# Two latent norms folded into the work behind them, and layer norm sums taken earlier, in a two-block transformer kernel on one core

## The chip, the cores and the metric

The kernel runs on one core of one Trainium2 chip. The metric is the device time of one execution in microseconds; less is better. Engines are named as in the profile: PE multiplies matrices (PEld loads its weights beside it), DVE and ACT work on vectors, POOL is the general engine, SP issues the DMAs. An operand is "f32" or "fp32r", the form in which a float32 value is split in a high part and a low part, so that one product is made of three matrix instructions.

## The reference, cut to what matters

Two blocks of two layers each are computed for 512 tokens of width 1024. The change touches the second block. Its layers are a state-space mixer with a gated feed-forward part, and a latent attention with a gated feed-forward part. Each of these four parts ends in a layer norm. In the latent attention both norms are root-mean-square norms:

```python
ckv_kr = h @ kv_down_proj                                  # 256 latent columns and 64 for the rotated key
c_kv   = rms_norm(ckv_kr[..., :256], kv_norm_g)
k_rope = apply_rope(ckv_kr[..., 256:], cos, sin)
k_nope, v = c_kv @ kv_up_k, c_kv @ kv_up_v                  # 8 heads of 128
c_q    = rms_norm(h @ q_down, q_norm_g)                     # 384 latent columns
q      = c_q @ q_up                                         # 8 heads of 128 + 64 rotated
scores = (q_nope @ k_nope.T + q_rope @ k_rope.T) * 192 ** -0.5
p      = softmax(where(key <= query, scores, -inf))
o      = (p @ v) @ out_proj
h      = layer_norm(alpha * h + o, g, b)                    # also behind the other three parts
```

A factor that belongs to one query (the reciprocal root of its mean square) multiplies all of that query's scores, so it may be applied to the scores as well as to the latents.

## The kernel before, in words

**Layout.** Activations lie transposed: 128 partitions hold 128 features, the 512 tokens are the columns, and 8 tiles make the width of 1024. A sum over features is therefore a product with a column of ones (`ones`), which gives one value per token, with tokens on the partitions; to spread a value per token over the partitions again, PE transposes it.

**Weights.** They stream through a ring of six slots. SP loads a slab, ACT copies it to the high part (`wh`, L486), POOL subtracts to get the low part (`wl`, L494), and PE multiplies three times (L520 to L522, the helper `product`). `split.hi(n)` and `split.lo(n)` do this for all slabs before number n, on ACT and POOL, at the place in the program where they stand. A slot is loaded again when the product that read it is done. Every engine works through its own list in program order and waits on semaphores; there is no other order.

**Latents.** Class `Latents` makes six tiles from the last layer norm's output: key-value latents 0 and 1, the rotary key (tile 2, its 64 rows twice), and query latents 0 to 2. Tiles 0 to 3 are the "head" of the crossing before, tiles 4 and 5 follow. DVE first computes the angles of sine and cosine, 16 small steps in all, then copies all six tiles out of PSUM. PE turns the rotary key (`rot2`, L1987), then comes the key-value norm and then the query norm, each as: square on ACT, sum by PE (L937), mean on DVE, power on POOL (L978), a diagonal matrix on DVE (L971), spread by PE (L962), multiply on DVE (L2059). After both, ACT makes the high parts and DVE the low parts of the five latent tiles and the rotary key, ACT writes zeros into the unused halves of the rotary key's tiles (L2015, L2016), and only behind all this does ACT convert the first slabs of the next stage (L486, four of them) and POOL make their low parts.

**LatentAttention.** Before its loop over eight heads PE projects, for the first head or pair, the rotary queries, the plain queries, turns the rotary part (L2162), then the keys and the values. A head is: scores (L520 and following), maximum on DVE (L2273), exponential on ACT (L2198, its scale a constant, its bias a value per partition), division by the sum on DVE (L2281), transposes of the probabilities on PE (L1507), and the products of the head before with the values. The projections of the next head stand between scores and transposes.

**Layer norm.** The `Dense` product before each layer norm is made of eight output tiles; the last one or two, the tail, are done in two halves of the tokens by a `Crossing`, so that the next stage can begin on the first half. To keep the squares small, tiles 0 and 1 give an estimate of the mean (`shift_sum`, L670, and `shift_spread`, L677), which is subtracted from all tiles. Then POOL adds the tiles up (L784, L775) in `gather`, ACT squares each (L711) into `tmp`, and DVE adds the squares up (L717) in `gather2`. `LayerCrossing.stat` (L1428) sums both over the features with PE; it waits for the tail's last square, which DVE adds at L1268, and for the last addition into `gather` (POOL's L775, DVE's L1418). `spread` (L1439) sends the result back, and DVE, ACT and POOL make the next stage's input from it (L1480, L1486, L1451, L1452, L1307). `STAT, SPREAD` say after which of the second half's weight rows in the tail these two stand. There are four such norms: behind the state-space mixer (three of its tiles are begun early, `early`, and its tail has two tiles), behind the first feed-forward part (tail of one tile), behind the latent attention (tail of two), and behind the last feed-forward part (tail of one).

## Time and profile before

| | |
|---|---|
| median of 3 runs | 2695.4 us (2692.55 to 2701.34) |
| the profiled execution's own time | 2694.61 us |
| its span in the profile | 2692.8 us |
| instructions | 32522 |
| PE busy | 2593.2 us, 96% of the span |
| POOL, DVE and ACT busy | 1175.0, 1376.2 and 1092.2 us |
| latents to first scores | 2096.3 to 2142.3 us of the span |
| layer norm behind the state-space mixer, tail to next stage | 1670.4 to 1699.4 us |
| layer norm behind the latent attention, tail to next stage | 2285.1 to 2306.4 us |

A row of a timeline gives the start in the span, the duration, the engine and line, the operation and its operands, a count where like instructions are merged, and in brackets how long the engine had been idle before and what ended that. A row of windows gives a stretch, then each engine's busy time in it, the granted PE clock as a share of 2.4 GHz (0.50 is the lower of its two levels, 1.2 GHz), the DMA engines' share and GB/s.

### The profile page before, as it was taken

How to read it: one execution, taken by the hardware profiler on the slowest of the kernel's cores; microseconds unless marked ns; L12 is line 12 of the kernel's file. 1: busy time of each engine (PE TensorE's matmuls, PEld its weight loads, DVE VectorE, ACT ScalarE, POOL GpSimd, SP SyncE). 2: the span in 40 equal slices, each digit the busy share in tenths (PEclk: the TensorE clock that was granted, in tenths of full speed). 3: DMA queues.
4: the chain of work that ended last, by engine and by line, in shares of the span. 5: the costliest groups of instructions: out<-in, count | busy, mean ns of one | idle time of the engine just before them, and what ended most of it. 6: DMA issues, size and time to landing. Idle time of an engine off the chain costs nothing.

```text
span 2692.8 us, 32522 instructions
## 1 busy us (share of the span) xinstructions
PE 2593.2 (96%) x13188; PEld 2187.5 (81%) x13188; DVE 1376.2 (51%) x2096; ACT 1092.2 (41%) x1885; POOL 1175.0 (44%) x634
## 2 busy tenths in 40 slices
PE   7999999999999999998999999899999899999997
PEld 5887988888889888896888887788888688888886
DVE  6775540523435505237574665661644574661654
ACT  5554531324225313324463554532434453542432
POOL 3333663444455644443334333544446214544443
PEclk9999999999999999998999999899999899999998
DMA  5222333332333333322223222223323112223332
GB/s 150 62 68 57 91 98 94 98 98 68 105 94 94 94 95 101 94 80 56 63 71 86 66 68 63 72 83 112 98 86 83 34 53 76 71 84 112 94 90 67
DMA packets 436005, 224.26 MB, mean 83 GB/s; under 512 B 14864, under 2 KB 433936, under 8 KB 435856
## 3 DMA queue, kind: packets, MB, share of 16 engines
q1 hardware_dynamic: 435856, 222.18, 29.0%
q8 instruction: 104, 1.70, 0.3%
q14 instruction: 45, 0.37, 0.0%
HBM read 219.01 MB, written 2.10 MB: 82 GB/s over the span
## 4 chain that ended last, share of the span: by engine, by line
PE 91%; DVE 5%; ACT 2%; POOL 1%; issue 1%; DMA 0%; SPq 0%; POOLq 0%; DVEq 0%; ACTq 0%
PE ps L520 28%; PE ps L522 28%; PE ps L521 28%; PE ps L2523 1%; PE ps L2509 1%; PE ps L1507 1%; PE ps L1428 1%; PE ps L2530 0%; PE ps L2511 0%; DMA xT<-in_xT 0%; ACT tmp L1664 0%; POOL sm L1821 0%; DVE acc L1486 0%; PE ps L2548 0%; DVE tmp L2766 0%
## 5 line engine op out<-in xcount | busy, mean ns | idle before, releaser
L494 POOL TENSOR_TENSOR wl<-stg,wh 128x1024 fp32r<-128x1024 f32 (+4 forms) x447 | 1003.7, 2252 | 1256.5 <-ACT wh L486 1249.8
L520 PE MATMUL ps<-hh,wh 128*128 128x512 f32 (+1 forms) x2308 | 868.7, 376 | 31.5 <-POOL wl L494 10.2
L522 PE MATMUL ps<-hh,wl 128*128 128x512 f32 (+1 forms) x2308 | 856.9, 371 | 0.0
L521 PE MATMUL ps<-hl,wh 128*128 128x512 f32 (+1 forms) x2308 | 856.3, 371 | 0.0
L486 ACT ACTIVATE wh<-stg 128x1024 fp32r<-128x1024 f32 (+4 forms) x447 | 435.6, 984 | 307.2 <-DMA stg<-in_mlp_w_down 109.2
L520 PEld LDWEIGHTS ps<-hh,wh 128*128 128x128 f32 x2308 | 436.8, 189 | 111.5 <-issue 17.2
L522 PEld LDWEIGHTS ps<-hh,wl 128*128 128x128 f32 x2308 | 436.4, 189 | 75.7
L521 PEld LDWEIGHTS ps<-hl,wh 128*128 128x128 f32 x2308 | 437.2, 189 | 72.3 <-issue 1.2
L520 PE MATMUL ps<-bh,wh 128*128 128x512 f32 (+1 forms) x1304 | 488.0, 374 | 2.4 <-DVE bl L1783 1.6
L522 PE MATMUL ps<-bh,wl 128*128 128x512 f32 (+1 forms) x1304 | 484.4, 371 | 0.0
L521 PE MATMUL ps<-bl,wh 128*128 128x512 f32 (+1 forms) x1304 | 484.3, 371 | 0.0
L520 PEld LDWEIGHTS ps<-bh,wh 128*128 128x128 f32 x1304 | 248.2, 190 | 45.0 <-DVE bl L1783 2.0
L522 PEld LDWEIGHTS ps<-bh,wl 128*128 128x128 f32 x1304 | 247.8, 190 | 42.3
L521 PEld LDWEIGHTS ps<-bl,wh 128*128 128x128 f32 x1304 | 248.0, 190 | 41.1
L884 DVE TENSOR_TENSOR bl<-tmp,bh 128x512 fp32r<-128x512 f32 x64 | 140.4, 2193 | 51.5 <-ACT bh L874 51.5
L1952 DVE SCALAR_TENSOR_TENSOR tmp<-ps,vec,tmp 128x511 f32<-128x511 f32 x88 | 66.0, 750 | 156.2 <-ACT tmp L1937 155.9
L1937 ACT ACTIVATE tmp<-ps,vec 128x512 f32<-128x512 f32 x88 | 67.7, 771 | 145.4 <-PE ps L522 145.2
L796 DVE COPY acc<-ps 128x512 f32<-128x512 f32 (+1 forms) x36 | 22.7, 632 | 182.2 <-PE ps L522 182.2
L869 ACT ACTIVATE tmp<-ps 128x512 f32<-128x512 f32 x64 | 38.1, 595 | 182.1 <-PE ps L522 182.1
L2766 DVE SCALAR_TENSOR_TENSOR tmp<-ps,vec,tmp 128x511 f32<-128x511 f32 (+2 forms) x96 | 71.9, 748 | 73.2 <-ACT tmp L2622 71.0
L881 DVE TENSOR_TENSOR tmp<-tmp 128x512 f32<-128x512 f32 x64 | 56.7, 886 | 94.0 <-ACT tmp L869 94.0
L1960 DVE SCALAR_TENSOR_TENSOR tmp<-tmp 128x512 f32<-128x512 f32 x44 | 91.2, 2073 | 0.0
(305 smaller groups left out, 2734.3 us busy)
## 6 DMA issues: line engine op xcount, KB each, us to landing
stg<-in_ffn_up SPq DMA_DIRECT2D x88, 512.0 KB, 3.8
stg<-in_mlp_w_up SPq DMA_DIRECT2D x64, 512.0 KB, 4.0
stg<-in_mlp_w_down SPq DMA_DIRECT2D x64, 512.0 KB, 4.0
stg<-in_ssd_in_proj SPq DMA_DIRECT2D x48, 512.0 KB, 3.9
stg<-in_attn_w_qkv SPq DMA_DIRECT2D x24, 512.0 KB, 4.1
stg<-in_conv_w_in SPq DMA_DIRECT2D x24, 512.0 KB, 3.7
stg<-in_ffn_down SPq DMA_DIRECT2D x32, 384.0 KB, 3.3
stg<-in_ffn_down SPq DMA_DIRECT2D x32, 320.0 KB, 3.1
```

Of the source, the lines that this page charges most:

```text
L486: act.activation(wh[:, slab.slot, w], stg[:, slab.slot, w], ACT.Copy).then_inc(s.hi_done, 1)
L494: pool.tensor_tensor(wl[:, slab.slot, w], stg[:, slab.slot, w], wh[:, slab.slot, w].bitcast(F32), ALU.subtract).then_inc(s.lo_done, 1)
L520: pe.matmul(po, lh, rh, start=start, stop=False)
L521: pe.matmul(po, lh, rl, start=False, stop=False)
L522: return pe.matmul(po, ll, rh, start=False, stop=stop)
L869: act.activation(tmp[:, t % 2, :], ps[:, t, :], ACT.Relu).then_inc(s.bank_free, 1)
L881: dve.tensor_tensor(tmp[:, 2 + t % 2, :], tmp[:, t % 2, :], tmp[:, t % 2, :], ALU.mult).then_inc(s.squared, 1)
L884: dve.tensor_tensor(tile(bl, 4 * i + t), tmp[:, 2 + t % 2, :], tile(bh, 4 * i + t).bitcast(F32), ALU.subtract).then_inc(s.hid_lo, 1)
L1937: act.activation(tmp[:, 3 * u + n, :], ps[:, 2 * u + n, :], ACT.Identity, bias=v("ffn_b", 2 * i + (self.b0 + n * FFN_T + u)), scale=self.t ...
L1952: dve.scalar_tensor_tensor(y[:, 1:T], x[:, 0:T - 1], self.taps(n, 1, i, u), y[:, 1:T], ALU.mult, ALU.add).then_inc(s.ffn_tap, 1)
L1960: dve.scalar_tensor_tensor(gate, th, 1.0, gate, ALU.add, ALU.mult).then_inc(s.ffn_silu, 1)
L2766: op = dve.scalar_tensor_tensor(y[:, d:T], x[:, 0:T - d], self.conv_col(i, n, 3 - d), y[:, d:T], ALU.mult, ALU.add)
```

## The change

- **Order and place of the latents.** Query tiles stay in PSUM banks 3, 1 and 2 (`Q_BANK`); only three tiles are copied. Tile 4 goes to bank 1 and so waits for two of the copies. The key-value sums stand inside tile 4's product, the key-value spread inside tile 5's; the spread is four transposes and no longer a diagonal matrix. The second half of the angle steps moves behind the copies.
- **Query norm.** The query latents are multiplied by the gain only. Their sums (`query_sums`) stand among the first projections. The factor of each query times 192 ** -0.5 becomes `q_scale`, a value per partition, which scales the exponential (and the maximum, by one `scalar_tensor_tensor` where a `tensor_scalar` stood).
- **Key-value norm.** The two normed tiles go to `bh`, `bl` tiles 6 and 7, so that they need not wait for the last product that reads `hh`.
- **Keys first.** The stage's slabs come as key, rotary, plain, value; PE's order is the same. ACT and POOL convert these four slabs (`split.hi`, `split.lo` up to `st.end + LEAD`) ahead of the query squares and behind the key-value power. The zeros of the rotary key's tiles come last on ACT.
- **Layer norm sums.** Squares go to two PSUM banks that are free instead of `tmp`. Without `early`, the estimate's sum stands inside tile 2's product and its spread at the head of tile 3's, and the order of shifts and squares becomes 2, 0, 1, 3. With `early`, POOL adds up four tiles only, and `stat` sums the other four with PE directly; `STAT, SPREAD` become 11 and 15. With two tail tiles, DVE's addition at L1418 falls away, and PE sums that tile too. So `stat` has six parts behind the state-space mixer and four behind the latent attention, where it had three; behind the feed-forward parts it keeps three.

```diff
+            st_mla = (stage("latent attention begin", 1, [(2, P, lambda i: key(0, 0)), (3, P, rope),
+                                                          (3, P, lambda i: nope(0, 0)), (2, 2 * P, value)]),
...
+            if self.shift and not self.early and n == 2 and x0 == 0:
+                return lambda j: self.shift_sum(pe) if j == 5 else None
+            if self.shift and not self.early and n == 3 and x0 == 0:
+                return lambda j: self.shift_spread(pe) if j == 0 else None
...
-            dve.tensor_tensor(gather2, gather2, tmp[:, 4 + k % 2, :], ALU.add).then_inc(s.sq_sum, 1)
+            dve.tensor_tensor(gather2, gather2, self.square_place(k), ALU.add).then_inc(s.sq_sum, 1)
...
+            self.f1 = dense.f0 + dense.summed()
+            if dense.early:
+                self.STAT, self.SPREAD = 11, 15
...
-        def tail_sum(self, dve, half, n):
-            super().tail_sum(dve, half, n)
-            if n < DT_ - 1:
-                k, cols = self.number(half, n), half_columns(half)
-                dve.wait_ge(s.gathered, self.f1 + half)
-                dve.tensor_tensor(gather[:, cols], gather[:, cols], acc[:, n, cols], ALU.add).then_inc(s.gathered, 1)
...
+            parts = [(gather, 0)] + [(acc[:, n, :], 0) for n in range(self.dense.summed(), DT_)] + [(gather2, 2)]
...
         def tensor(self, pe):
-            for pos in (4, 5):
-                multiply(pe, self.st, pos, 0, ps[:, pos, :], hh, hl, 0)
-            pe.wait_ge(s.kvq_copied, 4)
-            pe.matmul(ps[:, 3, :], rot2, acc[:, 2, :], start=True, stop=True).then_inc(s.kr_rot, 1)
-            self.kv.tensor(pe)
-            self.q.tensor(pe)
+            def rows(j):
+                if j == 5:
+                    for n in range(2):
+                        self.kv.stat(pe, n)
+            pe.wait_ge(s.kvq_copied, 2)
+            multiply(pe, self.st, 4, 0, ps[:, 1, :], hh, hl, 0, ready=rows)
+            pe.wait_ge(s.kvq_copied, 3)
+            pe.matmul(ps[:, 0, :], rot2, acc[:, 2, :], start=True, stop=True).then_inc(s.kr_rot, 1)
...
+                if j == 1:
+                    end.then_inc(s.lat_rows, 1)
+                if j == 2:
+                    self.spread(pe)
...
+            act.wait_ge(s.ang_done, 16)
+            act.activation(self.cos, tmp[:, 3, :], ACT.Sin).then_inc(s.tab_done, 1)
+            split.hi(act, self.st.end + LEAD)
+            wait_product(act, self.st, 4, 0)
...
+            for pos in range(3):
                 wait_product(dve, self.st, pos, 0)
                 dve.tensor_copy(acc[:, pos, :], ps[:, pos, :]).then_inc(s.kvq_copied, 1)
+            angle(1)
...
         def tensor(self, pe):
+            pe.wait_ge(s.kvq_lo, 4)
+            self.project_key(pe, 0)
+            pe.wait_ge(s.kvq_lo, 5)
+            pe.wait_ge(s.kr_done, 1)
+            self.project_rope(pe, 0)
+            self.lat.query_sums(pe)
+            self.project_nope(pe, 0)
+            self.turn(pe, 0)
+            pe.wait_ge(s.cross_var, self.lat.v0["cross_var"] + 2)
+            self.project_value(pe, 0)
             pe.wait_ge(s.kvq_lo, 7)
             pe.wait_ge(s.kr_zero, 4)
-            self.project_rope(pe, 0)
-            self.project_nope(pe, 0)
-            self.turn(pe, 0)
-            self.project_key(pe, 0)
-            self.project_value(pe, 0)
...
-                               bias=nm[:, n:n + 1], scale=self.scale,
+                               bias=nm[:, n:n + 1], scale=Latents.q_scale[:, b:b + 1],
```

## Rows read from the trace of the kernel before

**Rows 1.** The page's part 1: busy time, share, instructions.
```profile
PE 2593.2 (96%) x13188; PEld 2187.5 (81%) x13188; DVE 1376.2 (51%) x2096; ACT 1092.2 (41%) x1885; POOL 1175.0 (44%) x634
```
**Rows 2.** Waits of PE in the span: total us, times, longest.
```profile
PE ps L1428 <- DVE cb L1268: 18.5, 3, 11.8
...
PE ps L520 <- POOL wl L494: 10.2, 3, 8.1
```
**Rows 3.** Window from the last latent product to the first of the next stage.
```profile
2107.25:2131.50 24.25, 11.76 (x47) 8.50 (x46) 12.14 (x20) 9.99 (x18) 3.15 (x4) 0.57 0.02 6
```
**Rows 4.** Timeline of PE: tile 4's start, turn, two sums, first scores.
```profile
2096.33 0.40 PE L520 MATMUL ps<-hh,wh 128*128 128x512 f32 x1
...
2107.25 1.02 PE L1987 MATMUL ps<-acc,con 128*128 128x512 f32 x2
2108.11 1.84 PE L937 MATMUL ps<-con,tmp 128*128 128x1 f32 x16
...
2114.20 5.12 PE L937 MATMUL ps<-con,tmp 128*128 128x1 f32 x24
...
2142.34 0.40 PE L520 MATMUL ps<-bh 128*128 128x512 f32 x1
```
**Rows 5.** Timeline of DVE in the latents: end of the first angle, the copies.
```profile
2095.54 0.43 DVE L2042 TENSOR_SCALAR tmp<-tmp 128x512 f32<-128x512 f32 x1
...
2100.02 3.08 DVE L2046 COPY acc<-ps 128x512 f32<-128x512 f32 x5
```
**Rows 6.** Timeline of ACT and POOL: the four slabs of 1536 columns.
```profile
2129.76 1.76 ACT L486 ACTIVATE wh<-stg 128x384 fp32r<-128x384 f32 x4
...
2130.36 3.90 POOL L494 TENSOR_TENSOR wl<-stg,wh 128x384 fp32r<-128x384 f32 x4 [9.76 <-ACT wh L486]
```
**Rows 7.** Windows of the two stalled crossings: wait, then sums to next stage.
```profile
1678.75:1690.39 11.64, 0.00 (x0) 0.03 (x1) 8.05 (x7) 4.29 (x7) 11.64 (x6) 0.58 0.00 0
1690.39:1699.35 8.96, 8.96 (x46) 8.80 (x47) 2.76 (x10) 1.48 (x3) 1.57 (x2) 0.59 0.20 59
...
2293.12:2297.21 4.09, 0.00 (x0) 0.03 (x1) 3.49 (x4) 0.39 (x1) 4.09 (x3) 0.74 0.00 0
2297.21:2306.36 9.15, 9.15 (x47) 9.15 (x47) 2.96 (x11) 1.48 (x3) 1.56 (x2) 0.56 0.20 57
```
**Rows 8.** Timeline of the state-space crossing: first sum, POOL's last addition, DVE behind it.
```profile
1673.28 1.72 DVE L717 TENSOR_TENSOR cb<-cb,tmp 128x512 f32<-128x512 f32 x1
...
1685.21 1.25 POOL L775 TENSOR_TENSOR cb<-cb,acc 128x512 f32<-128x512 f32 x1
...
1686.50 2.55 DVE L1418 TENSOR_TENSOR cb<-cb,acc 128x256 f32<-128x256 f32 x1 [2.25 <-POOL cb L775]
```
**Rows 9.** Groups of DVE by form, 2060 to 2400: busy, mean ns.
```profile
L2286 DVE TENSOR_TENSOR bl<-ps,bh 128x512 fp32r<-128x512 f32 x16 | 11.0, 690 | 10.3 <-ACT bh L2210 8.1 <-ACT bh L2214 2.0
L717 DVE TENSOR_TENSOR cb<-cb,tmp 128x512 f32<-128x512 f32 x7 | 10.3, 1470 | 2.1 <-ACT tmp L711 2.1
```
**Rows 10.** Feed-forward crossing: PE's spread and next stage, then a window.
```profile
2066.79 0.43 PE L1439 MATMUL ps<-con,sm 128*128 128x128 f32 x2
...
2070.09 0.55 PE L520 MATMUL ps<-hh,wh 128*128 128x256 f32 x1 [1.94 <-DVE hl L1307]
...
2073.00:2074.00 1.00, 1.00 (x9) 1.00 (x9) 0.97 (x3) 1.00 (x3) 0.49 (x1) 0.88 0.00 0
```
**Rows 11.** Groups of ACT by form, 2060 to 2400: a pointer operand, none.
```profile
L2198 ACT ACTIVATE acc<-ps,sm 128x512 f32<-128x512 f32 x8 | 5.5, 688 | 17.9 <-DVE sm L2275 17.9
...
L2210 ACT ACTIVATE bh<-ps 128x512 fp32r<-128x512 f32 x8 | 4.8, 604 | 9.9 <-PE ps L522 9.9
```
**Rows 12.** A head in the loop: last division, first transpose.
```profile
2202.36 0.36 DVE L2281 TENSOR_SCALAR acc<-acc,sm 128x256 f32<-128x256 f32 x1
...
2205.10 0.38 PE L1507 MATMUL ps<-con,acc 128*128 128x128 f32 x2
```
**Rows 13.** The page's part 6: DMA issues, KB each, us to landing.
```profile
stg<-in_ffn_up SPq DMA_DIRECT2D x88, 512.0 KB, 3.8
```

More of the change, by code:

```diff
@@ L603, in begin, with summed @@
             self.early, self.banks = count, banks
+        def summed(self):
+            return TB if self.early else self.full
         def bank_of(self, n):
@@ L701, in square_order, with square_place @@
         def square_order(self):
-            return [2, 3, 0, 1] + list(range(4, self.full))
+            return ([2, 3, 0, 1] if self.early else [2, 0, 1, 3]) + list(range(4, self.full))
+        def square_place(self, k):
+            return ps[:, ((0, 1) if self.parts > 1 else (2, 3) if self.early else (5, 6))[k % 2], :]
         def shifted_square(self, act, n):
@@ L729, in shifted_vector, with shifted_vector_early @@
             self.shift_mean(dve)
+            dve.wait_ge(s.gathered, self.f0 + 1)
+            if self.early:
+                return self.shifted_vector_early(dve)
+            self.shift_tile(dve, 2)
+            self.shifted_out(dve, 2)
+            for n in (0, 1, 3):
+                self.shift_tile(dve, n)
+            for n, done in ((4, 2), (5, 0), (6, 1)):
+                self.shift_tile(dve, n)
+                self.shifted_sum(dve, done)
+            self.shift_tile(dve, 7)
+            for n in range(3, self.full):
+                self.shifted_out(dve, n)
+                self.shifted_sum(dve, n)
+        def shifted_vector_early(self, dve):
             for n in (2, 3):
@@ L1182, in bank_free @@
             pe.wait_ge(s.acc_done, SEED + d.before + max(users, default=1))
+            if d.shift and d.parts == 1 and not d.early:
+                for k in range(d.full - 2, d.full):
+                    if self.bank[half, n] == 5 + k % 2:
+                        pe.wait_ge(s.sq_sum, SEED + d.g0 + k + 2)
         def head_products(self, pe, half):
```

217 lines of the change are left out of this document (128 added, 89 removed).

## The prediction

> **What bounds the kernel.** I read the busy times first: PE is busy for 2593.2 of 2692.8 us [rows 1], so some 100 us of it is idle, and only work that PE does, its clock, or those gaps can give anything. The waits of PE come next. The largest is L1428, the layer norm's sums, 18.5 us in three places, of which 11.8 in one (4.1 is in the second [rows 7], so 2.6 in the last); the wait for the first low weights of the latent attention costs 8.1 [rows 2]. These are the places that the change touches. The windows then show what the waits cost beside the idle time: from 2107.25 to 2131.50 PE is busy for 11.76 of 24.25 us at a mean clock of 0.57 [rows 3], and behind both stalled sums it works at 0.59 and 0.56 [rows 7]. Everything else in these stretches has to be followed engine by engine, since each engine works in its own order. For the unit costs: 48 matrix instructions of 512 columns took 2107.25 - 2096.33 = 10.92 us [rows 4], so 0.2275 each, and I take half of this, about 0.12, for 256 columns. Sixteen instructions of one column took 1.84 us [rows 4]; they are two sums over four token blocks, so a tile's sum costs 0.92, and one part of a `stat` (two blocks) 0.46.
>
> **Part A, the latents.** I place each engine's list anew from 2096.33, where tile 4 starts now [rows 4]. DVE has done the first angle at 2095.97 [rows 5]; its copies cost 3.08 / 5 = 0.62 each, so banks 0 and 1 are out at 2097.3. PE waits 1.0 for them: a new stall. Then:
> - tile 4, 24 x 0.2275 = 5.46, the key-value sums inside it 1.84, the turn 0.86 (to the next start [rows 4]): 2105.5. Tile 5 with 0.4 for the transposes: 5.86, to 2111.35.
> - DVE has the second angle (2095.97 to 2100.02 [rows 5], so 4.0) behind the copies, at 2101.9. ACT stands at the cosine until then; behind it wait the four slabs (1.76 [rows 6]), which are high at 2104.4, and the squares of query tiles 0 and 1. POOL's power, an estimate of 1.0 us under the 1.25 of a whole operation [rows 8], and its four low slabs (3.90 [rows 6]) are done at 2107.8, before the keys need them. The 8.1 us wait is gone, since the slabs no longer stand behind the zeros.
> - The spread lands at 2108.0. DVE's chain to the low key-value tiles is two norms, two query lows and two lows, six operations of about 0.69 [rows 9]: 2112.2. PE waits 0.9. Keys 6 x 0.2275: 2113.65.
> - Rotary key cosine and sum, then the low part of query tile 2: DVE at 2114.2; PE waits 0.6. Rotary queries 2.05, query sums 3 x 0.92, plain queries 2.05: 2121.1. The third square can start only after the first sum, and the sum of tile 2 comes right behind it, with nothing lost.
> - ACT still has the third square and four zeros (0.55 each, an estimate from the 0.60 of a whole tile [rows 11]) ahead of the high keys and the raw rotary queries; these end at 2121.4, so the turn waits 0.4. Turn 0.9, values 24 x 0.12 = 2.9: 2125.3. DVE's rotation and the low rotary queries (four operations with two waits on ACT between) end at 2126.1. The scores start at 2126.2.
>
> Against 2142.34 [rows 4] that is 16.1 us less, of which 3.8 is left in five small stalls; without any stall it would be 20, the upper bound. The lower bound is the clock. In the trace a wait of 1.94 us let the clock fall, and it was back only in the window 2073 to 2074 [rows 10], three microseconds later, which costs 1.5. The one-column sums also do nothing to bring it up: at 2114.20 twelve logical sums took 5.12 us, with waits, and the window's mean stayed 0.57 [rows 3, 4]. I charge one such fall, 1.5: **A = -14.6**, between -18 and, with the clock low for most of the dense work, -5. Here a rule of the skill speaks for the better case. The Trainium skill, "TensorE: Matmul & The Clock Gate", What's actually happening, says the slow clock is the default and the engine's recent business releases it; if sums counted as business, A would be -16.1. The rows above do not show the sums releasing it.
>
> **Part B, the exponential's scale.** The exponential gets a second value per partition. Operations of 512 columns out of PSUM take 604 ns without one and 688 with one [rows 11], so 0.08 more for each of 32. The function differs between the two rows, which leaves the price of the second open: nothing at the least, and 0.69 if it doubled the operation. In the loop the last division ends 2.4 us before PE needs it (2202.72 against 2205.10 [rows 12]); four times 0.08 lies in that. Only in the last head, where no projection covers the chain, it shows: +0.3. If the cover were gone in all heads, it would be 2.6; doubled, the operations would take 2.8 a head, 0.4 beyond the cover, and 3 to 5 in all. The maximum's operation stays one instruction of one column. The slabs of the loop keep the order in which PE uses them.
>
> **Part C, the sums behind the state-space mixer.** Now POOL adds tiles 4 and 5 between its weight slabs and ends at 1686.46 [rows 8], DVE adds the tail tile only after that and beside POOL, in 2.55 us [rows 8], and PE starts the sums at 1690.39, 11.6 after it was there [rows 7]. After the change POOL's additions end with tile 3, two additions (1.3 each) and two slabs earlier; a slab of 1024 columns is 2.6 by rows 6 (3.90 for 1536), so before 1679, when PE is not there yet. DVE's sums read PSUM and cost 0.69 where they cost 1.47 [rows 9]. That the two slow each other is what the Trainium skill says too ("GPSIMD Engine Reference", Specifications: the interface is shared when DVE has two SBUF inputs); it changes no term here. What is late next is the tail's last square. DVE's sums begin at 1673.3 as now [rows 8]; the first four alternate with ACT's squares until 1676.0. ACT then copies four slabs (1.05 to 1.2 each, from 1.76 for 1536 columns [rows 6]) and squares tiles 4 and 5 (0.6 each), so it reaches the tail's first square at about 1680.6 to 1681.6. Two squares, two outputs and two sums of a half tile follow, and the last sum is in at about 1682.5. PE comes to `stat`, now after 12 of 16 rows, at 1680.6: a wait of 2. Then six parts instead of three, 2.8 us at full clock. POOL's four low slabs (2.5 each, begun with ACT's first copy at 1676.5) end at about 1686.5, and the power behind them lets the spread go at 1687.3 at the earliest, 1689.8 if the clock has fallen. From spread to the next stage it takes 2070.09 - 2066.79 = 3.3 [rows 10], and no tail rows are left to cover it. The next stage starts at 1692.5 with 1.5 either way, 6.9 before 1699.35 [rows 7]. The second half's `stat` adds 6 x 0.23 = 1.4, and I charge 1.0 for a low clock in the next stage: **C = -4.5**, between -2.5 and -7.4.
>
> **Part D, the sums behind the latent attention.** The estimate moves ahead by most of a tile's product (24 x 0.2275 = 5.5), so shifts, squares and sums keep pace with PE, and DVE's 2.5 us addition of the tail falls away. The last slab that ACT copies needs the slot of tile 5, free at 2285.1, and 3.8 for its DMA [rows 13]; it stands ahead of the tail's square, which so comes at 2290.1. I get the last sum at 2292.3, before PE is there at 2293.1 [rows 7]. So the 4.1 us wait is gone, and with it the low clock behind it. From there: four parts 1.84, four rows 1.45, waiting for the spread 0.35, then 3.3: 2300.0, against 2306.36 [rows 7], -6.4; the second half's additional part costs 0.5. **D = -5.9**, between -4 (the copy late by one DMA) and -6.5.
>
> **Part E, the two feed-forward norms.** The estimate's sum after 15 of a tile's first 18 instructions finds POOL's first addition done: 15 x 0.2275 = 3.4 us after the tile before it, in which DVE needs 0.69 and POOL 1.25, with one slab of 2.0 at most in its way. Nothing waits for the squares there but the tail, whose wait is on its own half. Zero; if POOL were late by a slab, half a microsecond each.
>
> **The sum.** -14.6 + 0.3 - 4.5 - 5.9 = -24.7. The profiled execution took 2694.6 us, 1.8 outside its span, so 2669.9; the median of the runs is 0.8 above it. I say 2670.
>
> **Rivals.**
> - *The clock never falls in the new stretches.* A -16.1, C -7.4, D -5.9, +0.3: -29.1, 2666. For it: none of the new stalls in A is above 1.0, where the fall in the rows came with 1.94 [rows 10]. Against: 4.6 us of one-column sums and several stalls in 30 us. Chance 0.17. The rule of the Trainium skill quoted in part A ("TensorE: Matmul & The Clock Gate", What's actually happening) would lead here.
> - *The clock stays low through the latents and the state-space crossing.* Some 15 us of dense work in A takes nearly twice as long, partly inside the stalls: A -5, C -2.5, D -5.9: -13, 2682. For it: before, the mean was 0.57 for 24 us [rows 3]. Against: PE was then busy half the time, now 0.85 of it. Chance 0.15.
> - *The sums' gain is taken up by POOL.* `power` stands on POOL behind the four low slabs, and if these run until 1690 as now (POOL is busy for all 11.64 [rows 7]), the spread waits where `stat` waited. C is then 0 to +1.4, D -2: with A and B at -14.3 that is some -15.5, 2679. Against: POOL loses two additions and starts earlier. Chance 0.08.
> - *Slower.* The exponential with a pointer scale costs much more than the rows of the other functions tell, and the softmax chain, which has 2.4 us of cover per head, comes to set the loop. To lose 8 us in all it must eat 24.7 + 8 over eight heads, 4.1 each behind the cover of 2.4: 1.6 us more per exponential, where the pointer rows say 0.08. It gives 2703 at that point. Chance 0.02.
> - *The latents' gain is real but small for another reason*, such as ACT's cosine wait holding slabs and squares longer than I placed them; around 2678. Chance 0.05, and 0.53 for the forecast.
>
> **Range.** A measurement of this kernel tells 0.3%, 8 us, from no change. The forecast's own range is 2666 to 2676. The first rival lies at its lower edge and the next ones reach 2682; from 2661 to 2683 no more than 0.1 is left out on either side. Faster by over 0.3% 0.95, within it 0.03, slower 0.02.
>
> **What would show it.** The scores of the first head start near 2126 to 2128, with no PE wait on L494 above 1 us before them and small waits ahead of tile 4, keys, rotary queries and turn. The two L971 and L962 groups are gone there. The first `stat` of the state-space crossing waits about 2 us, that of the latent attention not at all; the last one, 2.6 us, stays. L717 takes 0.7 us. The exponentials take 0.08 more, and the distance from head to head stays. The prediction is wrong if the granted clock is 0.5 in the dense work of A, if ACT is what `stat` waits for by 5 us, or if a head becomes longer.

## The result, and the profile of the changed kernel

The changed kernel takes 2670.95 us (median of five, four of them from 2670.64 to 2673.07) against 2695.4 us. The fifth was in a slow state, 3250.5 us at a mean granted clock of 0.75; without it the median is 2670.9, and nothing below is taken from it. The ratio is 0.9906 with a 95% interval of 0.9892 to 0.9921: 0.9% faster. 2670 was forecast. Measured a second time beside the kernel before, the ratio was the same (below).

The page of the profiled execution, head and busy times (before: [rows 1]):

```profile
span 2671.2 us, 32576 instructions
PE 2595.1 (97%) x13220; PEld 2189.2 (82%) x13220; DVE 1348.6 (50%) x2085; ACT 1094.3 (41%) x1885; POOL 1168.2 (44%) x632
```

PE is busy for 1.9 us more than before; its idle time fell from 99.6 to 76.1 us, and the span is 21.6 us shorter. The changed kernel's waits of PE, some of the rows (before: [rows 2]):

```profile
PE ps L523 <- DVE hl L1334: 6.2, 6, 2.6
...
PE ps L1452 <- DVE cb L1295: 4.2, 2, 2.6
...
PE ps L523 <- DVE bl L2406: 3.5, 3, 1.8
```

The layer norm's sums, 18.5 us of waiting before, cost 4.2, and the 8.1 us for the first low weights of the latent attention are gone. In the latents, the timeline of PE has these waits (before, one of 8.1 us and a clock of 0.57 beside it: [rows 2 to 4]):

```profile
2111.06 0.50 PE L523 MATMUL ps<-bh,wh 128*128 128x512 f32 x1 [0.59 <-DVE bl L2133]
...
2113.05 0.50 PE L523 MATMUL ps<-hh,wh 128*128 128x512 f32 x1 [0.32 <-DVE hl L2090]
...
2120.17 0.70 PE L2253 MATMUL ps<-tmp,con 128*128 128x512 f32 x1
...
2124.97 0.47 PE L523 MATMUL ps<-bh 128*128 128x512 f32 x1 [0.80 <-DVE bl L2399]
```

The turn (2120.17) waits for nothing; the keys, the rotary queries and the scores wait 0.59, 0.32 and 0.80 us. Tile 4, ahead of these rows, waits 0.86. The windows of the same kernel over the latents, and over the crossing behind the latent attention:

```profile
2095.25:2110.30 15.05, 14.19 (x70) 11.49 (x70) 9.18 (x17) 9.05 (x15) 4.91 (x5) 1.00 0.25 66
2110.30:2124.97 14.67, 12.94 (x75) 10.37 (x75) 8.20 (x15) 7.90 (x15) 1.39 (x2) 1.00 0.17 45
2271.00:2296.00 25.00, 23.84 (x199) 23.27 (x198) 13.26 (x38) 13.19 (x24) 13.77 (x13) 1.00 0.22 63
```

PE is busy for 14.19 of 15.05 us and 12.94 of 14.67, at full clock throughout. Behind the latent attention the clock holds too. It does not hold behind the state-space mixer. First PE's timeline there:

```profile
1684.36 0.58 PE L1452 MATMUL ps<-con,cb 128*128 128x1 f32 x4 [1.62 <-DVE cb L1295]
1684.80 2.42 PE L1452 MATMUL ps<-con,acc 128*128 128x1 f32 x16
1687.08 0.99 PE L1452 MATMUL ps<-con,cb 128*128 128x1 f32 x4
1687.93 0.56 PE L523 MATMUL ps<-bh,wh 128*128 128x256 f32 x1
...
1690.63 0.63 PE L1463 MATMUL ps<-con,sm 128*128 128x128 f32 x2
...
1694.33 0.55 PE L523 MATMUL ps<-hh,wh 128*128 128x256 f32 x1 [2.64 <-DVE hl L1334]
```

Then the windows of the same stretch (before: [rows 7]):

```profile
1678.49:1682.70 4.21, 4.21 (x36) 4.04 (x34) 1.82 (x4) 4.06 (x6) 4.21 (x2) 1.00 0.03 8
...
1684.36:1687.95 3.59, 3.59 (x25) 3.59 (x25) 0.00 (x0) 0.00 (x0) 3.50 (x2) 0.74 0.03 9
1687.95:1694.33 6.38, 3.74 (x17) 3.37 (x18) 2.71 (x10) 1.48 (x3) 0.71 (x1) 0.50 0.29 82
1694.33:1702.24 7.91, 7.91 (x48) 7.91 (x49) 4.26 (x12) 5.52 (x11) 2.20 (x3) 0.66 0.00 0
1702.24:1708.12 5.88, 5.88 (x39) 5.88 (x39) 2.59 (x8) 3.02 (x5) 4.75 (x6) 0.71 0.00 0
```

PE waits 1.62 us for the last sum; then 24 one-column instructions take 3.7 us. In the middle of them, at 1686.0, the clock falls to 0.50 for 13.65 us, and at 1703.1 for 3.41 us more.

**How runs are compared below.** The total moves by several microseconds from one execution to the next, and most of that lies early. The profiles show it: VectorE's MEMSET that opens the layer norm behind the state-space mixer starts anywhere between 1654.20 and 1665.34 us in thirteen profiles, although almost no kernel changes anything ahead of it (the two that do are named; the changed kernel and the one before run the same instructions up to there). From there on, two executions of the changed kernel agree within 0.2 us in every stretch. So I read each profile from that MEMSET (M) on, in stretches between instructions that all kernels have: to the first variance of the first feed-forward crossing (F1), its second (F2), the first row maximum of the latent attention (X), the second variance behind it (V), the end. All numbers are differences of start times in us, the last is taken to the end of the span. There is one profile of each kernel and two of the changed one, so a difference that comes from one row alone can be one of execution.

| kernel | M to F1 | F1 to F2 | F2 to X | X to V | V to end | M to end |
|---|---|---|---|---|---|---|
| before | 408.68 | 10.65 | 68.19 | 167.33 | 381.43 | 1036.28 |
| changed | 406.08 | 10.06 | 52.21 | 162.96 | 381.42 | 1012.73 |
| changed, again | 406.07 | 10.07 | 52.23 | 162.95 | 381.40 | 1012.72 |
| lat_only | 408.67 | 10.76 | 52.21 | 168.71 | 380.88 | 1021.23 |
| sums_only | 406.09 | 10.06 | 68.17 | 161.27 | 380.86 | 1026.45 |
| nm_pointer | 405.95 | 10.08 | 53.34 | 161.90 | 381.49 | 1012.76 |
| const_scale | 406.06 | 10.08 | 52.19 | 159.71 | 381.46 | 1009.50 |
| tail_order | 403.86 | 11.15 | 54.97 | 164.08 | 381.23 | 1015.29 |
| fill_idle | 402.66 | 10.08 | 52.20 | 162.90 | 381.48 | 1009.32 |
| zeros_first | 406.06 | 10.07 | 51.86 | 163.22 | 381.39 | 1012.60 |
| pool_late | 405.93 | 10.07 | 53.33 | 158.22 | 381.42 | 1008.97 |
| split_sums | 405.44 | 10.08 | 52.20 | 163.11 | 381.43 | 1012.26 |
| combined | 402.37 | 10.07 | 51.83 | 161.04 | 380.80 | 1006.11 |

Between the first two rows lie 23.55 us: 2.60 behind the state-space mixer, 0.59 in the feed-forward crossing, 15.98 in the latents, and 4.37 in the heads and the crossing behind them. The 2 us by which the two spans differ less (21.6) were lost ahead of M.

### The profile page after: what moved, and what is told of

It is laid out like the page before. It is cut to its first block, busy times and chain, and to the rows that moved or that the text cites. A ratio compares the mean times of both kernels' runs of the same rounds, so it can differ in the third digit from the quotient of the medians.

```text
span 2671.2 us, 32576 instructions
## 1 busy us (share of the span) xinstructions
PE 2595.1 (97%) x13220; PEld 2189.2 (82%) x13220; DVE 1348.6 (50%) x2085; ACT 1094.3 (41%) x1885; POOL 1168.2 (44%) x632
## 4 chain that ended last, share of the span: by engine, by line
PE 92%; DVE 5%; ACT 1%; POOL 1%; issue 1%; DMA 0%; SPq 0%; DVEq 0%; POOLq 0%; ACTq 0%
PE ps L523 29%; PE ps L525 28%; PE ps L524 28%; PE ps L2622 1%; PE ps L2608 1%; PE ps L1452 1%; PE ps L1531 1%; PE ps L2629 0%; DVE acc L1510 0%; PE ps L1554 0%; DMA xT<-in_xT 0%; PE ps L2610 0%; DVE acc L1504 0%; ACT tmp L1688 0%; POOL sm L1845 0%
## 5 line engine op out<-in xcount | busy, mean ns | idle before, releaser
L523 PE MATMUL ps<-hh,wh 128*128 128x512 f32 (+2 forms) x2292 | 864.2, 377 | 29.3 <-DVE hl L1102 11.2
L525 PE MATMUL ps<-hh,wl 128*128 128x512 f32 (+2 forms) x2292 | 851.8, 372 | 0.0
L524 PE MATMUL ps<-hl,wh 128*128 128x512 f32 (+2 forms) x2292 | 851.4, 371 | 0.0
L523 PEld LDWEIGHTS ps<-hh,wh 128*128 128x128 f32 (+1 forms) x2292 | 435.0, 190 | 107.8 <-issue 21.3
L523 PE MATMUL ps<-bh,wh 128*128 128x512 f32 (+1 forms) x1320 | 493.8, 374 | 2.9 <-DVE bl L1807 1.6
L525 PEld LDWEIGHTS ps<-hh,wl 128*128 128x128 f32 (+1 forms) x2292 | 434.8, 190 | 74.8
L524 PEld LDWEIGHTS ps<-hl,wh 128*128 128x128 f32 (+1 forms) x2292 | 435.5, 190 | 71.6 <-issue 1.2
L525 PE MATMUL ps<-bh,wl 128*128 128x512 f32 (+1 forms) x1320 | 489.8, 371 | 0.0
```

Source lines behind the costliest of these rows:

```text
L523: pe.matmul(po, lh, rh, start=start, stop=False)
L524: pe.matmul(po, lh, rl, start=False, stop=False)
L525: return pe.matmul(po, ll, rh, start=False, stop=stop)
```

## The experiments

### One part of the change alone

Two kernels, each the kernel before with one part of the diff. `lat_only` has the stage order, `Latents` and `LatentAttention`; `sums_only` has `Dense`, `LayerCrossing` and their places for squares. The core of each:

```diff
 # lat_only
-                               bias=nm[:, n:n + 1], scale=self.scale,
+                               bias=nm[:, n:n + 1], scale=Latents.q_scale[:, b:b + 1],
...
 # sums_only
+            if dense.early:
+                self.STAT, self.SPREAD = 11, 15
```

> The kernel before with only the latent and attention edits (keys first, query norm in the exponential's scale); the layer norms' sums as before. Theory A (the ledger of the two profiles holds part by part, and the parts add): 16.1 us less to the first scores, 1.5 to 1.8 us given back in the heads, so 14.3 to 14.6 us under the kernel before, near 2681. Rival (part of what the ledger puts down to the latents was granted clock that happened to be better in that one execution, or the gains overlap with those of the sums): at most 12 us, 2683 or more. In the trace: second stall of the latents gone, first scores 16 us earlier, the crossing behind the state-space mixer as before.

> The kernel before with only the edits of the layer norms' sums; latents and attention as before. Theory A (ledger): 2.6 us behind the state-space mixer and 6.0 behind the latent attention, 8.6 in all, near 2686.8. Rival 1 (the prediction's own terms, 4.5 and 5.9): 10.4, near 2685.0. Rival 2 (feed-forward crossings lose or gain too because squares now go through PSUM banks): another 0.5 us either way beyond 8.6, seen in those crossings' windows.

Measured: `lat_only` 2687.26 us, ratio to the kernel before 0.9952 (0.9937 to 0.9967), which is 12.9 us; `sums_only` 2690.78 us, ratio 0.9970 (0.9959 to 0.9980), 8.1 us. The intervals, 9 to 17 and 5 to 11 us, hold both the theory and the rival of each, so the totals decide nothing. From M to the end they are 15.05 and 9.83 us shorter than the kernel before, 24.9 together, where the whole change has 23.55. The latents' stretch is 15.98 shorter in `lat_only`, as in the whole change, and the stretch behind the state-space mixer 2.59 shorter in `sums_only`. So the parts add within 1.4 us, and most of that lies in the last stretch, V to end, where both took 0.55 less and the changed kernel, which has both edits, did not; up to V they add to 23.8 against 23.5. `lat_only` changes nothing in that stretch. In `sums_only` 2.59 and 6.06 us are the 8.6 of theory A, and the 0.59 in the first feed-forward crossing is what its second rival allowed for. Two further readings follow. The heads with the crossing behind them take 1.38 us more in `lat_only` than before and 1.69 more in the changed kernel than in `sums_only`: that is what part B cost in these executions, the clock included. And the same stretch puts part D at 6.06 in `sums_only`, and at 5.75 between `lat_only` and the changed kernel.

### The maximum's operation in the last head

Part B was forecast at 0.3 us. VectorE's timeline of the changed kernel in the last head shows two operations of one column that take over 1 us; the group of all 32 has a mean of 222 ns. Below them GpSimd's slab operations at that time:

```profile
2221.83 1.07 DVE L2371 SCALAR_TENSOR_TENSOR sm<-sm 128x1 f32<-128x1 f32 x1
...
2224.05 1.20 DVE L2371 SCALAR_TENSOR_TENSOR sm<-sm 128x1 f32<-128x1 f32 x1
...
2225.49 0.16 DVE L2371 SCALAR_TENSOR_TENSOR sm<-sm 128x1 f32<-128x1 f32 x1
...
2220.50 2.39 POOL L497 TENSOR_TENSOR wl<-stg,wh 128x1024 fp32r<-128x1024 f32 x1
2222.84 2.40 POOL L497 TENSOR_TENSOR wl<-stg,wh 128x1024 fp32r<-128x1024 f32 x1
```

Both long operations end with a slab: 2221.83 + 1.07 = 2222.90 and 2220.50 + 2.39 = 2222.89; 2224.05 + 1.20 = 2225.25 and 2222.84 + 2.40 = 2225.24. Without a slab beside it the same operation takes 0.16. PE, which needs what follows from it for the transposes, waits 2.05 us:

```profile
2228.21 1.90 PE L1531 MATMUL ps<-con,acc 128*128 128x128 f32 x10 [2.05 <-DVE acc L2378]
```

Three kernels ask whose fault that is.

```diff
 # nm_pointer: one tensor operand, the query scale as a scalar operand
-                dve.scalar_tensor_tensor(nm[:, n:n + 1], mx[:, n:n + 1], -1.0, Latents.q_scale[:, b:b + 1], ALU.mult,
-                                         ALU.mult).then_inc(s.m_negmax, 1)
+                dve.tensor_scalar(nm[:, n:n + 1], mx[:, n:n + 1], Latents.q_scale[:, b:b + 1], -1.0, ALU.mult,
+                                  ALU.mult).then_inc(s.m_negmax, 1)
 # const_scale: the maximum times -self.scale, and in the exponential
-                               bias=nm[:, n:n + 1], scale=Latents.q_scale[:, b:b + 1],
+                               bias=nm[:, n:n + 1], scale=self.scale,
 # pool_late: GpSimd in the attention stage
+            split.lo(pool, self.st[2].end + lead(self.st[2]) - 2)
+            pool.wait_ge(s.m_combined, 4 * HEADS)
             lo_stage(pool, self.st[2])
```

> The changed kernel, with the row maximum's operation written as one tensor-scalar operation: the maximum times the query scale as the scalar operand, times minus one; one tensor operand in SBUF instead of two, same result. Theory A (an operation with two SBUF tensor operands waits for GpSimd's slab operations, which run beside it in the last head): the 1.07 and 1.20 us operations fall to 0.15 to 0.2, the last head gets shorter by about 1 us on VectorE, and the time falls by 0.5 to 1.5 us against the changed kernel, to 2669.5 to 2670.5. Rival (the long records are a coincidence of that execution, or hidden behind the exponentials): same time as the changed kernel, 2671, within 0.3 us.

> The changed kernel with the constant scale in the exponentials and in the maximum's operation, so the query norm's factor is left out of the softmax. Theory A (the pointer scale costs 0.09 us in each exponential, of which only the end of a head and of the loop sees any, and the maximum's operation costs 1 us in the last head): 1.3 to 1.8 us under the changed kernel, near 2669.3. Rival 1 (the prediction's term, 0.3 us): 2670.7. Rival 2 (the 1.8 us that the heads took more are clock or upstream delay, not the operations): exponentials at 0.69 us again, the heads' stretch no shorter.

> The changed kernel; GpSimd waits with the last two of the three slabs that it splits beside the last head until that head's normalising is through. Theory A (a VectorE operation from SBUF to SBUF that starts beside a GpSimd slab operation is held until that one ends, as 2221.83 + 1.07 and 2224.05 + 1.20 in the changed kernel fall on the ends of slab operations): the maximum's operations take 0.16 us in the last head, the wait ahead of its transposes is 1.0 instead of 2.05 us, and with the better clock 1.0 to 1.6 us less; nothing waits for the two slabs. Rival (the operation is slow for another reason, as its pointer operand): still over 1 us, nothing gained; or the output projection waits for the late slabs and gives it back.

Measured: `nm_pointer` 2675.04 us, ratio to the kernel before 0.9911 (0.9891 to 0.9932); `const_scale` 2673.26 us, ratio 0.9912 (0.9892 to 0.9931); `pool_late` one run, 2675.61 us, with M at 1664.83, late by itself. Against the changed kernel at 0.9906 none of these totals tells anything, and none of the gains that were expected of them shows in them; the stretches tell more. The last head of `nm_pointer`, VectorE and then GpSimd:

```profile
2228.78 0.21 DVE L2371 TENSOR_SCALAR sm<-sm 128x1 f32<-128x1 f32 x1
...
2231.88 1.70 DVE L2378 TENSOR_SCALAR acc<-acc,sm 128x512 f32<-128x512 f32 x1
...
2230.91 2.38 POOL L497 TENSOR_TENSOR wl<-stg,wh 128x1024 fp32r<-128x1024 f32 x1
```

The maximum's operation no longer waits for a slab, as theory A has it: 0.21 us beside GpSimd. But 3 us later the first normalising of the probabilities, 0.49 us in the changed kernel, is caught instead and takes 1.70, until 0.29 after the slab's end at 2233.29. PE's wait ahead of the transposes is 2.38 us instead of 2.05, so the operations' gain didn't reach PE. The stretch X to V is 1.06 shorter all the same; PE's first scores of that head ran at full clock here and not in the changed kernel, so no part of it is put down to the edit. The same rows of `pool_late`:

```profile
2228.06 0.16 DVE L2371 SCALAR_TENSOR_TENSOR sm<-sm 128x1 f32<-128x1 f32 x1
2229.22 0.56 DVE L2369 TENSOR_REDUCE sm<-ps 128x1 f32<-128x384 f32 x1 [1.00 <-PE ps L525]
2229.82 0.16 DVE L2371 SCALAR_TENSOR_TENSOR sm<-sm 128x1 f32<-128x1 f32 x1
...
2231.01 0.49 DVE L2378 TENSOR_SCALAR acc<-acc,sm 128x512 f32<-128x512 f32 x1
...
2232.96 2.36 POOL L497 TENSOR_TENSOR wl<-stg,wh 128x1024 fp32r<-128x1024 f32 x1 [5.06 <-DVE acc L2378]
...
2232.93 1.31 PE L1531 MATMUL ps<-con,acc 128*128 128x128 f32 x10 [1.02 <-DVE acc L2378]
```

With the slabs held back, the unchanged operation with its two SBUF inputs takes 0.16 us throughout that head, the normalising 0.49, and PE waits 1.02 us instead of 2.05, as expected. X to V is 4.74 us shorter than in the changed kernel, more than the 1.0 to 1.6 expected. Not all of that is the edit's: already ahead of it, from 2218.20 to 2222.53, the changed kernel's clock was 0.61, and `pool_late`'s stayed at 1.00. In `combined`, where the clock fell there again, the same edit is left with 1.9 us, so its worth lies between 1.9 and 4.7. That stretch of `combined` is also no longer than that of `sums_only` (161.04 against 161.27), with two falls of 3.41 us of the clock in both: with the slabs out of the way the new scale costs nothing there. And in all eight profiles in which PE waits 2.0 us or more ahead of those transposes, the clock is then low for 6.8 us or longer, in the other five for 3.4 or not at all; so I read part B's price as the longer wait and the low clock that comes with it. The wait varies from one execution to the next: in `tail_order`, which changes nothing there, the two operations took 2.19 and 1.84 us and PE waited 3.64.

In `const_scale`, which leaves the query norm's factor out of the softmax and so computes something else, the exponentials take 0.69 us again where the changed kernel has 0.78 (512 columns), and the wait ahead of the transposes is 0.98. X to V is 3.25 us shorter than in the changed kernel and 1.56 shorter than in `sums_only`, in which the same operations stand: there the clock fell a second time. So the two prices of B can't be had from this kernel to better than one fall of the clock.

The Trainium skill, "SBUF — State Buffer", Who interferes with whom, states the rule that I should have weighed: a DVE operation with both inputs in SBUF contends with GpSimd's reads, a copy or `tensor_scalar` can too in a two-port mode, and whoever comes second is blocked until the first has finished. The rows agree, to 0.01 us in the first two cases; for the normalising, with one tensor input, they agree with its second half.

### The clock behind the state-space mixer

```diff
 # tail_order, ScalarE and VectorE
-            split.hi(act, self.split_at + self.ahead())
+            early = self.dense.early
+            split.hi(act, self.split_at + self.ahead() - (1 if early else 0))
             for n in self.tail:
                 self.tail_square(act, 0, n)
+            split.hi(act, self.split_at + self.ahead())
...
+            if self.dense.early:
+                for n in self.tail:
+                    self.tail_out(dve, 0, n)
+                for n in self.tail:
+                    self.tail_sum(dve, 0, n)
 # fill_idle, 12 ahead of the first stat and 18 ahead of the next stage
+            for _ in range(count):
+                pe.matmul(po, wh[:, slot, 0:po.shape[0]], self.dense.xh[:, 0, 0:256], start=True, stop=True)
 # split_sums
-                        self.stat(pe, 1)
+                        self.stat(pe, 1, (0, 1, 2))
+                    if half == 0 and j == 2 and self.dense.shift and self.dense.early:
+                        self.stat(pe, 1, (3, 4, 5))
```

> The changed kernel; in the crossing behind the state-space mixer VectorE first evicts both tail tiles' first halves and then adds their squares, and ScalarE squares them ahead of its last slab copy. Theory A (the wait of 1.62 us ahead of the first sums is this chain alone, and with it goes the half clock in which the 24 one-column products and 12 rows ran): wait under 0.5 us, sums in 2.4 to 2.8 us instead of 3.71, clock 1.00 up to the spread, next stage's first product 3 to 4.5 us earlier after the crossing's start, and about 3 us less in all. Rival (the half clock comes from the sums themselves, one-column products, not from the wait): the wait goes, the sums still take 3.7 us, next stage 1.2 to 1.6 us earlier.

> The changed kernel; in the crossing behind the state-space mixer TensorE runs 12 products of 256 columns into a free bank ahead of the first sums, and 18 ahead of the next stage's first product; their results are overwritten or never read. No other engine is changed. Theory A (the clock fell because TensorE stood idle there, and the fall is what made this term smaller than predicted): clock 1.00 through the crossing, sums 2.4 to 2.8 us instead of 3.71, next stage's products and the second sums at full clock, 2 to 4 us less up to the second half's variance and the stage behind it. Rival (one-column products lower the clock whatever stands before them, or the chain over VectorE and GpSimd sets the times): clock falls all the same or the times stand still, at most 0.5 us less.

> The changed kernel; the second sums behind the state-space mixer are issued as 12 one-column products behind the next stage's second tile and 12 behind its third instead of 24 in a row, and the 24 of the query's squares in the latents as 8 ahead of each of the three column blocks of the first content query. Seen so far: right behind the 24 in a row of the second sums the clock fell in every run with the new sums (the stretch from the second variance to the next crossing takes 362.1 us, 360.65 before), and behind the 24 of the query in three runs of eight (1.1 to 2.8 us). Theory A (a long unbroken row of one-column products counts for the clock as little work): with the rows broken up the clock stays at 1.00 behind both, the stretch from the second variance falls from 362.1 to 360.7 to 361.2 us, the latents' stretch is 52.2. Rival (the stretch is longer because the second variance now comes earlier against the same products, or the clock fell from the idle time ahead): 362 us again, or what is saved behind the sums is lost because the variance comes 0.7 us later.

One run each: 2671.25, 2670.10 and 2671.28 us. The first two edits also reached the one crossing of this kind in the first block, ahead of M; there the filling cost 2.7 us. Their windows from the last tail products on, first `tail_order`:

```profile
1678.70:1681.51 2.81, 2.81 (x25) 2.81 (x26) 0.00 (x0) 0.19 (x1) 2.81 (x3) 1.00 0.53 156
1681.51:1688.65 7.14, 3.45 (x17) 2.78 (x17) 4.47 (x10) 1.48 (x3) 2.84 (x2) 0.53 0.26 73
```

The wait is 0.21 us instead of 1.62, and the sums take 2.81 instead of 3.7. Yet right behind them the clock is down (0.53), without any idle time ahead of them but that 0.21. M to F1 is 2.2 us shorter, not 3, and the next stage starts 1.4 us earlier, not 3 to 4.5; theory A was right on the wait and on the sums and wrong on the clock and on the start, which came as the rival has it. `fill_idle`:

```profile
1683.23:1684.86 1.63, 1.44 (x14) 1.26 (x12) 1.03 (x3) 0.39 (x1) 1.63 (x2) 1.00 0.99 292
1684.86:1687.66 2.80, 2.80 (x25) 2.80 (x26) 0.00 (x0) 0.00 (x0) 2.80 (x2) 1.00 0.01 3
1687.66:1692.99 5.33, 4.35 (x35) 3.97 (x35) 3.11 (x10) 1.48 (x3) 1.49 (x2) 1.00 0.34 98
1692.99:1699.48 6.49, 5.93 (x49) 5.73 (x50) 4.27 (x12) 5.52 (x11) 2.20 (x3) 1.00 0.01 3
1699.48:1705.22 5.74, 5.74 (x37) 5.74 (x37) 2.60 (x8) 3.03 (x5) 4.75 (x6) 0.70 0.00 0
```

Thirty instructions whose results nobody reads, and the clock stays at 1.00 for 16 us; M to F1 is 3.42 us shorter than in the changed kernel. The edit touches no other engine, so I read this as what the 13.65 us of low clock cost in this stretch. The last row shows that the fall behind the second sums is still there, and ahead of it PE had not been idle for more than 0.56 us at a time. `split_sums` breaks up those sums:

```profile
1693.05:1698.51 5.46, 5.46 (x27) 5.46 (x27) 4.26 (x12) 5.06 (x11) 2.21 (x3) 0.51 0.00 0
1698.31:1702.51 4.20, 4.20 (x38) 4.20 (x38) 0.00 (x0) 0.65 (x2) 0.00 (x0) 0.99 0.00 0
1702.51:1706.15 3.64, 3.06 (x25) 2.86 (x25) 2.59 (x8) 2.23 (x5) 2.86 (x5) 1.00 0.00 0
```

Behind the two groups of 12 the clock is 1.00, where it was 0.71 behind the 24 in a row. All nine profiles with the 24 second sums in a row have that fall, and neither of the two with groups (`split_sums`, `combined`). The stretch from the second variance to F1 falls from 362.13 to 360.03, as theory A has it; but the second variance comes 1.4 us later against the first, and M to F1 is only 0.64 shorter: the rival's second half is true as well. The fall at the first sums, which this edit leaves in a row, is still there. The query sums were broken up too, but their stretch of 52.20 us is what most profiles have without that, so it shows nothing.

### The last stall of the latents, and the clock there

```diff
-            self.q.square(act, 2, ps[:, self.Q_BANK[2], :])
             for e in range(2):
                 other = slice(64 - 64 * e, 128 - 64 * e)
...
+            self.q.square(act, 2, ps[:, self.Q_BANK[2], :])
...
+            self.rope(dve, 0)
             self.low(dve, 0, 1, self.QN, ps[:, 5, :])
-            self.rope(dve, 0)
             self.rope_low(dve, 0)
```

> The changed kernel; in the latents ScalarE writes the four zero halves of the rotary keys ahead of the third query square, and VectorE takes the first query's low part between the two parts of the rotary work. Theory A (the last stall, 0.80 us before the first scores, hangs on this chain): stall 0 to 0.2 us, first scores 0.6 to 0.8 us earlier, nothing else moves. Rival (the square is later now and the query sums wait for it): a new wait ahead of the sums' last third, first scores no earlier.

One run, 2673.47 us. The latents' stretch is 0.35 us shorter and the wait ahead of the scores still 0.73: ScalarE's part of the chain was taken away, and behind it the rotation on VectorE now stands behind the turn on PE, which is only 0.28 us earlier; the rotation is 0.37 earlier, and so are the scores. Half a miss; the theory took one link for the chain.

The table holds something else. F2 to X is 51.8 to 52.2 us in eight profiles with the new latents, and 53.3, 53.3 and 55.0 in `nm_pointer`, `pool_late` and `tail_order`, which change nothing there. The windows of `nm_pointer` over the query sums, the plain queries, and what follows:

```profile
2122.01:2124.74 2.73, 2.73 (x26) 2.72 (x25) 0.00 (x0) 1.72 (x3) 0.00 (x0) 1.00 0.26 72
2124.61:2127.56 2.95, 2.95 (x12) 2.38 (x12) 0.76 (x2) 2.27 (x5) 0.26 (x1) 0.75 0.00 0
2127.56:2132.29 4.73, 4.72 (x27) 3.48 (x25) 2.94 (x5) 1.53 (x3) 0.75 (x1) 0.80 0.10 29
```

In the changed kernel the plain queries took 2.33 us at 1.00. Here the clock fell behind the 24 one-column instructions; the last idle time of PE, 0.34 us, lay 2.2 us ahead of them. That is the fall for which the prediction charged 1.5 us; it costs 1.1 to 2.8 and comes in three of the nine profiles in which these 24 stand in a row. Whether the edits elsewhere brought it or the execution did is not shown.

### All together, and the changed kernel once more

`combined` is the changed kernel with the edits of `tail_order`, `zeros_first`, `pool_late` and `split_sums`, and 8 filling instructions ahead of the first spread and 18 ahead of the next stage.

> The changed kernel with: the tail's order (evictions first, squares ahead of the last slab copy), 8 filling products ahead of the first spread and 18 ahead of the next stage, second sums and query sums broken up, zeros first, and GpSimd's two slabs held back in the last head. The crossing's edits touch the crossing behind the state-space mixer alone here. Theory A (the effects add, as they lie in different stretches): from the state-space mixer's tail to the end 8 to 10 us less than the changed kernel in a run in which the latents' clock doesn't fall, about 0.997 of the changed kernel, near 2662. Rival (the crossing's edits take the same wait away twice and GpSimd's gain was luck of timing): 3 to 5 us less.

> The changed kernel once more, beside the combined one on one chip. Theory A: median 2669 to 2676, ratio to the kernel before 0.990 to 0.992; most of the spread from one run to the next lies ahead of the state-space mixer's tail, where nothing is changed. Rival (the first measurement was lucky): 0.993 or more.

Measured on one chip: `combined` 2665.83 us, ratio to the kernel before 0.9881 (0.9866 to 0.9895); the changed kernel again 2672.29 us, ratio 0.9906 (0.9892 to 0.9920). `combined` is faster than the kernel before; against the changed one the two ratios make 0.9975, but their intervals overlap at the edge, so the totals alone don't separate them. Its slowest run, 2669.59 us, is level with the fastest of the changed kernel, 2669.58, and from M to the end its profile has 6.6 us less. Of these, 3.7 lie behind the state-space mixer, 0.4 in the latents, 1.9 in the heads, and 0.6 in the last feed-forward crossing, which it doesn't touch. Expected were 8 to 10 by the theory and 3 to 5 by the rival, so both missed. The clock fell again in the last head, twice. And the edits behind the state-space mixer, which gave 2.2, 3.4 and 0.6 us one by one, gave 3.7 together (with 26 filling instructions instead of 30): there the rival is right that they take away the same time twice. The second measurement of the changed kernel confirms the first.

## Why the prediction was right, point by point

- **Part A** (-14.6, measured -15.98). The order and the stalls were right: 0.86, 0.59, 0.32, 0 and 0.80 us of waiting in the changed kernel's timeline for the 1.0, 0.9, 0.6, 0.4 and 0.9 forecast. The 1.5 us charged for a fall of the clock were not due in this execution; in three others such a fall came.
- **Part B** (+0.3, measured +1.4 to +1.7). The exponential's price, 0.08 from the pointer rows, was right: 0.09. The step that failed is "The maximum's operation stays one instruction of one column". It does, but it now has two inputs in SBUF and waits for GpSimd's running slab. At 0.16 us alone and 1.07 and 1.20 beside a slab, it makes PE's wait ahead of the last transposes 2.05 us where `const_scale` has 0.98 and `pool_late`, with the operation as it is, 1.02. The prediction named a longer head as a sign of being wrong, and for the last head that sign came.
- **Part C** (-4.5, measured -2.60). The wait of 2 (1.62), the six parts, and the next stage 6.9 us earlier (6.97) came out, the last although the sums took 3.7 us and not 2.8. Behind that start the forecast gives back 1.4 for the second sums and 1.0 for the clock, 2.4 in all; 4.37 were given back. The term that was too small is "I charge 1.0 for a low clock in the next stage": the clock stayed at 0.50 for the first 5.3 us of that stage, and the second sums were followed by another fall. `fill_idle` prices the low clock from the first sums on at 3.4. The bounds of C, 2.5 and 7.4, don't follow from its terms either: a start 6.9 earlier with 1.5 either way, less 1.4 and less 0 to 1.0, gives 3.0 to 7.0; the measured 2.60 lies inside the stated bounds and outside these.
- **Part D** (-5.9, measured -5.8 to -6.1). Right in size and in its steps; `stat` waits for nothing at 2277.38.
- **Part E** (0, measured -0.59). In the first feed-forward crossing the clock did not fall behind an idle time of 1.93 us, where it had fallen behind 1.94 [rows 10]. That is so in ten of eleven profiles with the new sums and in neither with the old. The length of the idle time doesn't decide it: `after_again` has no fall behind 1.94 us, and `lat_only` has one behind 1.93. Why is open.
- **The sum** was -24.7 and came to -23.55 from M on; 2 us that nothing in the change explains were lost ahead of M. The errors of B and C, 3.0 to 3.3 together, and the 2.0 of A and E largely cancel. That the total came within 1 us of 2670 is therefore in part luck; the order, the stalls and part D are not.
- **The rivals.** The clock never fell in A but did in C, so neither of the first two rivals came in whole. POOL did not take up the gain: the spread waited for the half-clock rows. The exponentials did not slow the loop.

## What to carry to other kernels

Replacing VectorE's or GpSimd's additions by one-column products on TensorE can take away the wait, but a long row of them can leave the clock low behind it. Breaking such a row up among wide products kept the clock up here, and most of the 2.1 us that this gave were lost again because the sums then end later (0.64 net); so price the sums and the next few microseconds at either clock before choosing. When an edit gives a small VectorE operation a second SBUF input, look for GpSimd operations that run beside it where no slack covers it: the price is not the operation's but the rest of GpSimd's. And where the total scatters by more than the effect, compare stretches between instructions that both kernels have, and take more than one profile where a fall of the clock may come or not.

## What the runs showed of the hardware that I had not expected

- The clock can fall with hardly any idle time ahead: with 0.21 us just ahead in `tail_order` and 0.34 a little earlier in `nm_pointer`, both times behind 24 one-column instructions in a row. Behind the rows of 16 in the changed kernel, of the key-value sums and at 2277.38, it did not. Nor is the row alone enough: in `fill_idle` the same 24, with 12 wide instructions where PE had waited, ran at 1.00 and were followed by 1.00.
- Two executions of the changed kernel agree in every stretch from M to the end within 0.2 us, falls of the clock included. Yet in `nm_pointer` and `pool_late` falls came and went in stretches that their edits don't touch; in both M was late, at 1665.34 and 1664.83, so the execution may be the cause as well as the edit. One profile of an edit can be off by 1 to 3 us for this alone.
- A VectorE operation of one column was held beside GpSimd for 1.04 us, in `tail_order` for 2.0, and an operation of 512 columns with one tensor input for 1.2.
